# Latent attention: the low parts of the exponentials move from GpSimd to the vector engine

## The reference, cut to what matters

```python
q = split_heads(rms_norm(c_q, mla_cq_norm) @ mla_w_uq, MLA_HEADS)      # 8 heads, 96 wide
kv = split_heads(rms_norm(c_kv, mla_ckv_norm) @ mla_w_ukv, MLA_HEADS)
k_nope, v = jnp.split(kv, [MLA_NOPE_DIM], axis=-1)
k = jnp.concatenate([k_nope, k_rope_h], axis=-1)
q = rms_norm(q, mla_q_norm)
k = rms_norm(k, mla_k_norm)
# the last 32 of the 96 columns of q and k are rotated by position
s = jnp.einsum("bhqd,bhkd->bhqk", qb, kb) * scale
p = jax.nn.softmax(jnp.where(mask, s, -jnp.inf), axis=-1)
outs.append(jnp.einsum("bhqk,bhkd->bhqd", p, v))
```

## Time and profile before

| | |
|---|---|
| runs of the kernel | 2476.98, 2477.01, 2480.07 us, median 2477.01 |
| the profiled execution's own time | 2482.53 us |
| its span, first to last instruction | 2480.8 us |
| TensorE busy | 2385.0 us (96%), 14064 matmuls |
| vector engine busy | 1410.4 us (57%), 2063 instructions |
| ScalarE busy | 956.7 us (39%) |
| GpSimd busy | 506.2 us (20%), of it low parts of the latent attention 108.1 us (112 instructions) |
| mean granted TensorE clock | 0.976 of full speed |
| latent attention, its 14 x 8 steps | 1203 to 1624 us |

### The profile page before, as it was taken

The page is one execution under the profiler, slowest core; times in us unless marked ns, Lnnn a source line. Parts: engine busy times, 40 slices in busy tenths (PEclk is TensorE's granted clock), DMA queues, the critical chain, the costliest instruction groups (busy, mean ns, idle before and its releaser), DMA issues. The chain is left out here.

```text
span 2480.8 us, 36883 instructions
## 1 busy us (share of the span) xinstructions
PE 2385.0 (96%) x14064; PEld 2113.8 (85%) x14064; DVE 1410.4 (57%) x2063; ACT 956.7 (39%) x1619; POOL 506.2 (20%) x632
## 2 busy tenths in 40 slices
PE   7999999999999999999999999989989999999999
PEld 7999999999998978878788887778868888887887
DVE  8666555555556475563555555554386666556553
ACT  6333323333434544543343343453353333333331
POOL 0033200000023342330233333432301222000000
PEclk8999999999999999989999999999999999999999
DMA  5366633375421000000111111044514665328652
GB/s 192 132 204 210 204 129 108 132 281 189 163 108 30 27 6 21 26 17 27 46 38 42 38 37 50 14 148 168 189 51 151 227 213 180 129 73 299 211 197 99
DMA packets 132699, 298.00 MB, mean 120 GB/s; under 512 B 10096, under 2 KB 57072, under 8 KB 129216
## 3 DMA queue, kind: packets, MB, share of 16 engines
q1 hardware_dynamic: 132544, 295.88, 34.4%
HBM read 206.99 MB, written 88.72 MB: 119 GB/s over the span
## 5 line engine op out<-in xcount | busy, mean ns | idle before, releaser
L1083 DVE TENSOR_TENSOR f_w_lo<-f_rw,f_w_hi 128x1024 fp32r<-128x1024 f32 x154 | 196.6, 1277 | 219.8 <-ACT f_w_hi L595 219.8
L846 PE MATMUL f_ps<-u_hi,f_w_hi 128*128 128x260 f32 (+1 forms) x1056 | 280.5, 320 | 10.3 <-DVE u_lo L1021 10.1
L846 PE MATMUL f_ps<-u_lo,f_w_hi 128*128 128x260 f32 (+1 forms) x1056 | 280.4, 320 | 0.0
L846 PE MATMUL f_ps<-u_hi,f_w_lo 128*128 128x260 f32 (+1 forms) x1056 | 280.2, 320 | 0.0
L846 PE MATMUL f_ps<-f_far_hi,f_w_hi 128*128 128x260 f32 (+1 forms) x792 | 214.3, 325 | 18.1 <-DVE f_ev L1099 8.7
L595 ACT CAST f_w_hi<-f_rw 128x1024 fp32r<-128x1024 f32 x154 | 160.9, 1046 | 163.7 <-PE f_ps L846 159.8
L846 PE MATMUL f_ps<-f_far_lo,f_w_hi 128*128 128x260 f32 (+1 forms) x792 | 213.1, 324 | 0.0
L846 PE MATMUL f_ps<-f_far_hi,f_w_lo 128*128 128x260 f32 (+1 forms) x792 | 213.0, 324 | 0.0
L846 PEld LDWEIGHTS f_ps<-u_hi,f_w_hi 128*128 128x128 f32 x1056 | 176.1, 190 | 25.6 <-issue 11.2
L846 PEld LDWEIGHTS f_ps<-u_lo,f_w_hi 128*128 128x128 f32 x1056 | 176.0, 190 | 13.9
L846 PEld LDWEIGHTS f_ps<-u_hi,f_w_lo 128*128 128x128 f32 x1056 | 175.6, 189 | 13.7
(11 more groups left out here) (393 smaller groups left out, 5974.7 us busy)
## 6 DMA issues: line engine op xcount, KB each, us to landing
f_rw<-in_gu SPq DMA_DIRECT2D x88, 512.0 KB, 4.1
f_rw<-kept_dsum SPq DMA_DIRECT2D x32, 704.0 KB, 5.4
f_rw<-kept_hid SPq DMA_DIRECT2D x33, 520.0 KB, 5.6
f_rw<-in_down SPq DMA_DIRECT2D x24, 704.0 KB, 4.2
f_rw<-kept_hid SPq DMA_DIRECT2D x33, 512.0 KB, 5.4
h_in<-in_wd SPq DMA_DIRECT2D x11, 1024.0 KB, 6.7
kept_dsum<-h_in SPq DMA_DIRECT2D x44, 256.0 KB, 3.2
h_out<-in_wd SPq DMA_DIRECT2D x11, 1024.0 KB, 7.4
```

The costliest lines, as they stand in the source:

```text
L846: last = nc.tensor.matmul(out[:, b, 0:N], w[:, c], u[:, b * N:(b + 1) * N], start=(j < 3 and k == 0 and i == 0), stop=(k == 3 and i == 2), ...
L1083: nc.vector.tensor_tensor(slot(w_lo, st), src, slot(w_hi, st).bitcast(F32), ALU.subtract).then_inc(wlo_done, 1)
```

## The change

GpSimd's program keeps the Newton steps of the next head and loses the low parts. The vector engine makes each low part directly behind its high part, after a wait on the semaphore that the high part raises. `weigh` and the exponentials wait for the same semaphores as before. The number of operations is the same.

```diff
-            def head(p, h, more=True):
-                for w in range(NW):
-                    if more and w < NU:
-                        newton_step(p, h + 1, w)
-                    n = ST_UNITS[w][4]
-                    upto(pool, phi_done, NW, p, h, w + 1)
-                    nc.gpsimd.tensor_tensor(p_lo[:, w % 2, 0:n], p32[:, w % 2, 0:n],
-                                            p_hi[:, w % 2, 0:n].bitcast(F32), ALU.subtract).then_inc(plo_done, 1)
-
             def pair(p, last=False):
-                head(p, 0)
-                head(p, 1, more=not last)
+                for u in range(NU):
+                    newton_step(p, 1, u)
+                if not last:
+                    for u in range(NU):
+                        newton_step(p, 2, u)
...
                     nc.vector.tensor_copy(p_hi[:, w % 2, 0:n], p32[:, w % 2, 0:n]).then_inc(phi_done, 1)
+                    upto(dve, phi_done, NW, p, h, w + 1)
+                    nc.vector.tensor_tensor(p_lo[:, w % 2, 0:n], p32[:, w % 2, 0:n],
+                                            p_hi[:, w % 2, 0:n].bitcast(F32), ALU.subtract).then_inc(plo_done, 1)
                     if more:
                         roots(p, h + 1, w)
                         prepare(p, h + 1, w)
```

## The result

The changed kernel took 2513.85 us (median of four runs, 2509.93 to 2516.94) beside 2478.54 us for the kernel before on the same chip (four runs, 2476.98 to 2482.32): 1.0139 times as long, with a 95% interval of 1.0117 to 1.0162, that is 29 to 40 us more. The forecast was 2500.6 us and a range up to 2512: slower was right, the size was not, and the median lies 1.85 us above the range.

What follows compares the result with a forecast made beforehand. TensorE was taken as the bound, idle half a microsecond per head. Six heads at 3.07 us (18.4), plus 5.6 for the seventh, less 0.4 for the last, gave +23.6 on 2477.0: 2500.6 us, range 2487 to 2512.

Steps and rivals of the forecast that it cites:

- steps 12 and 13: End of a head: maxima rows leave later, TensorE already waits for their DMA; 0.33 us a head after a faster high part.
- step 1: Newton step ahead of the broadcast: delay 0.61 us against slack 0.57, cost 0.04 us a head.
- step 2: Scaled keys ahead of the next key projection: delay 0.47 us against slack 0.05, cost 0.42 us a head.
- steps 3 and 4: Scaled keys ahead of the key projection, twice more, without slack: delays 0.34 and 0.21 us, cost 0.55 a head.
- step 5: Newton step ahead of the broadcast: delay 0.72 us against slack 0.14, cost 0.58 us a head.
- steps 7 and 8: Two maxima delay the next high part by 0.11 us, then 0.72 more; TensorE already waits for the third maximum: cost 0.83.
- steps 9 to 11: Maxima ahead of matmuls that reuse their bank: first slack 0.54 us, costs 0.18, 0.09 and 0.05, together 0.32 a head.
- steps 0 and 6: First delay of 0.72 us hidden behind TensorE's sums; second 0.72 cancelled by 0.9 us regained on the shortened 272-column product.
- The relief wins: Rival: the shortened 272-column product brings 0.9 us per head, 6.4 in seven heads, so 2470 us; chance 0.04.
- All of it is hidden: Rival: the 53 us of delays slide into the vector engine's 160.9 us of idle time, so 2477 us; chance 0.08.
- Nothing is hidden: Rival: every low part's delay is paid, 53 us, so 2530 us; chance 0.10 for more than forecast, up to this.
- half of it: Rival: TensorE's queue or overlapping waits leave a third to two thirds of the sum, 2485 to 2492 us; chance 0.13.

Runs made afterwards that it cites:

- steps 7 to 12 alone: Kernel before, with only the low parts of these six steps of each head moved to the vector engine behind their high parts: 2497.37 us, stage 435.04 (+14.2).
- steps 1 to 5: Kernel before, with only the low parts of these five steps of each head moved to the vector engine behind their high parts: 2498.51 us, stage 438.59 (+17.7).

## Why the direction was right, and the size was not

**What bounds the kernel** was right. TensorE has next to no idle time in the first six heads; with no low parts at all the stage gains 1.3 us, with all of them behind the high parts it loses 31.0. The argument that the idle 160.9 us lie ahead of the high part and not behind it is shown: the work costs 3.7 us put ahead, 31.0 put behind.

**The unit costs** were right: 0.69, 0.58, 0.44, 0.31 and 0.18 us forecast, 692, 576, 443, 309 and 175 ns measured; a step's delay of 0.72; the 272-column product from 1.34 to 0.43 where 0.44 was said. The upper bound of 1.1 us for 512 columns wasn't reached.

**The terms of the sum**, in the third head, whose 3.07 became 3.70:

| term | forecast | measured | held |
|---|---|---|---|
| steps 12 and 13, rows by DMA (shows in step 0) | 0.33 | 0.26 | yes |
| step 1 (shows in steps 1 and 2) | 0.04 | 0.07 | yes |
| step 2 (shows in step 3) | 0.42 | 0.44 | yes |
| steps 3 and 4 (show in 4 and 5) | 0.55 | 0.54 | yes |
| step 5 (shows in step 6) | 0.58 | 0.63 | yes |
| steps 7 and 8 (show in 8 and 9) | 0.83 | 0.75 | yes |
| steps 9 to 11 (show in 10 to 12) | 0.32 | 1.01 | no |

The first six are within 0.08 us each and 2.69 of 2.75 together. Read step by step, slack by slack, the method worked; and steps 0 and 6, forecast as hidden and as cancelled, cost 0.5 us in all heads together when made alone.

**The step that failed is the pricing by one head**, "The first six heads run the same plan and take about 57 us each, so this head stands for six": that head's sum of 3.07 us took its last term, the 0.32 for steps 9 to 11, too small (0.64 measured, and 1.01 with a late start), and the six took 3.10 to 5.39 us more, 24.2 together in place of 18.4. The seventh took 6.87 in place of 5.6, the last gave back 0.06 in place of 0.4. The 7.4 us that the sum lacks are, by the head table and the runs:

- *Steps 9 to 11, about 2 us.* I took the slack off the delay and no more. A wait that appears where there was none costs about 0.1 us beyond it. Steps 10, 11 and 12 grew by 0.29, 0.21 and 0.14 us (0.51 less a late start of 0.37), forecast 0.18, 0.09 and 0.05. The timeline of step 10, TensorE, after:

```profile
1367.11 0.46 PE L2656 MATMUL mla_bank<-mla_k_hi,mla_q_hi 96*128 96x400 f32 x1
...
1367.40 0.39 PE L73 MATMUL mla_bank<-u_hi,mla_gate_hi 128*128 128x512 f32 x1
```

and its weight load, then the load of the same matmul before and the matmul behind it:

```profile
1367.11 0.19 PEld L2656 LDWEIGHTS mla_bank<-mla_k_hi,mla_q_hi 96*128 96x128 f32 x1 [0.29 <-DVE mla_mpart L2813]
```

```profile
1360.83 0.19 PEld L2662 LDWEIGHTS mla_bank<-mla_k_hi,mla_q_hi 96*128 96x128 f32 x1
...
1361.20 0.39 PE L73 MATMUL mla_bank<-u_hi,mla_gate_hi 128*128 128x512 f32 x1
```

The matmul behind the late one starts 0.29 us after it, where before it was 0.18 (1361.02 in the earlier trace rows, the next at 1361.20). Before, the load ran 0.19 us ahead of its matmul; after, both start together, so the load is no longer covered by the matmul ahead, and that is handed on too. The steps grow alike, by 0.29, 0.21 and 0.15 us, in the kernel with steps 7 to 12 alone, which has no late starts there. 0.32 us a head for seven heads.

- *Late starts in the vector engine's loop, about 3.2 us.* 0.37 us in each of heads 3 to 6 and 1.7 in the fifth beside. These are gone with the loop written out, with 2.9 us measured, one new late start of 0.37 included. The kernel before has no such rows, and nothing in it hinted at them. Their cause isn't settled.

- *The second head of a pair, about 1.1 us.* 0.37 us in heads 2, 4 and 6, in steps 8 and 9, from `finish`. The timeline in the sixth head after:

```profile
1544.84 0.43 DVE L2804 TENSOR_TENSOR mla_q_lo<-mla_x,mla_q_hi 96x272 fp32r<-96x272 f32 x1
1545.30 0.69 DVE L2877 TENSOR_TENSOR o_mla<-mla_bank,mla_rden 64x512 f32 x1
```

and the same pair in the third:

```profile
1359.91 0.43 DVE L2804 TENSOR_TENSOR mla_q_lo<-mla_x,mla_q_hi 96x272 fp32r<-96x272 f32 x1
1360.26 0.68 DVE L2877 TENSOR_TENSOR o_mla<-mla_bank,mla_rden 64x512 f32 x1
```

Finishing the second head writes rows 64 and up (its `rows` begin at `VD * (h % 2)`), and starts 0.03 us behind the end of the one before instead of 0.08 us ahead of it. That stood in the kernel before as well, but behind slack; behind a late high part it reaches TensorE. The two heads of a pair differ in the same way in the kernel with steps 7 to 12 alone (0.34 us in steps 8 and 9), and not in the one with steps 1 to 5. That this start alone makes up the 0.37 wasn't tested.

- *The half clock in the seventh head, about 1.0 us*, by step 3 of that head at either clock (6.36 and 5.32 us). The head was charged 5.6 and took 6.9.

- *The last head, 0.34 us.* The gain of 0.4 was credited, -0.06 measured: its step 0 waits for the maxima rows as every head's does (+0.20), which the sum left out. To the other side, the first head has no such wait within it (0.26 less than a second head).

Together 2.2 + 3.2 + 1.1 + 1.0 + 0.3 = 7.8, less 0.3 in the first head: 7.5 of 7.4.

**The rivals.** *The relief wins*: the product was shortened as it said, and TensorE did nothing with it; without any low part the gain is 1.3 us. *All of it is hidden*: false where the change puts it, all but true elsewhere (+3.7 and +4.7). The rule that work between two engines which aren't the busiest changes nothing failed here by 31 us, and moving two calls within one of them gained 5. *Nothing is hidden* is false by steps 0 and 6, +0.5 us for 16 low parts with 0.72 us of delay each, 11.5 in all, against 6.4 that the shorter product could give back. Its size, though, was nearer than *half of it*, which assumed gains in TensorE's queue that do not show: where delay was handed on, it grew.

**The signs that the prediction named** came out so: 112 subtractions, 0.69 us at 512 columns; GpSimd 100 us less for 108 said, the 108.1 of its low parts gone and the rest of its work 8.0 us longer in that execution, 5.7 of it in its additions of the feed-forward parts; scaled keys and queries 7.9 us more in seven heads, 1.1 a head (1.0 said); maxima 12.8, 1.8 a head (1.1 said); the rows' DMA 2.2, 0.3 (0.3 said); roots 7.1 us, 1.0 a head (0.6 said), with 0.9 in the seventh. The first six heads 59.3 to 62.6 us for 60.

## What to carry to other kernels

An engine's idle time has a place: before putting work on it, ask what stands behind the new instruction in that engine's program and when the busiest engine needs it, and put the work behind that, or in front of a wait that is long anyway. The same reading finds gains in the order as it is: due results that stand behind a wait for the busiest engine can go ahead of it. A wait in the table is not yet a gain: look whether the step gets shorter, for another wait may stand behind the one that goes. When one iteration is priced for many, look at each kind of iteration (the other parity, the ones with less filler work, the loop's edges), and add about 0.1 us for each wait that is new on an engine that had none.

## What was not expected of the hardware

- A wait on the vector engine's own last result costs 0.10 us where another operation could overlap (0.07 to 0.09 us of overlap, and 0.03 behind the end), up to 0.30 in places (0.22 behind the end); 112 of them cost 8.3 us of stage, 3.4 us of half clock in the seventh head included.
- GpSimd's three-column operation took 0.53 us instead of 0.20 beside a 0.69 us subtraction of the vector engine that had started 0.21 us before it.
- TensorE's granted clock fell to half for 3.4 to 13.7 us in the seventh head of six profiles out of fourteen, in both of the changed kernel behind a wait of about 1.06 us, and not in the one where the waits of that head were shortened. A seventh head with waits of 1.26 and 0.96 us had none. What decides it is open.
- With all low parts in the vector engine's loop, one operation of the fifth head started 2.4 to 3 us late, with nothing to wait for that the profile shows, in six profiles out of six; in the changed kernel four more started 0.36 us late. Written out, the program shows one of 0.36 us. Left open.
